# Rotary embedding in a decoder layer on one core: the two halves exchanged by a VectorE shuffle in place of a TensorE product, the cosine product on GpSimd

## What is computed

```python
def partial_rotary(x, pos):
    half = ROT_DIM // 2          # 8
    inv_freq = ROPE_THETA ** (-jnp.arange(half, dtype=jnp.float32) / half)
    ang = pos.astype(jnp.float32)[:, None] * inv_freq[None, :]
    cos, sin = jnp.cos(ang)[:, None, :], jnp.sin(ang)[:, None, :]
    xr = x[..., :ROT_DIM].astype(jnp.float32)
    x1, x2 = xr[..., :half], xr[..., half:]
    rot = jnp.concatenate([x1 * cos - x2 * sin, x2 * cos + x1 * sin], -1).astype(x.dtype)
    return jnp.concatenate([rot, x[..., ROT_DIM:]], -1)
```

## Time and profile before

| what | us |
|---|---|
| median of 3 runs | 1114.33 |
| lowest and highest | 1111.66, 1116.53 |
| profiled execution, its own time | 1120.03 |
| its span in the trace | 1118.0 |
| PE, DVE, ACT, POOL busy | 1066.5, 469.8, 225.4, 216.9 |
| rotation on DVE, first to last operation | 187.47 to 218.32 |

### The profile page before, as it was taken

How to read it: one execution, slowest core, us unless ns; L and a number is a source line. 1 busy time by engine, 2 the same in 40 slices (tenths; PEclk the granted TensorE clock), 3 DMA queues, 4 the chain that set the end, 5 groups by cost and what they waited for, 6 DMA issues and landing times. The chain is left out here.

```text
span 1118.0 us, 20957 instructions
## 1 busy us (share of the span) xinstructions
PE 1066.5 (95%) x8584; PEld 701.7 (63%) x8584; DVE 469.8 (42%) x939; ACT 225.4 (20%) x376; POOL 216.9 (19%) x193
## 2 busy tenths in 40 slices
PE   9999999999999899996999999999999999999980
PEld 8999998899997678874444444444444444444430
DVE  2799999800125728475232322121222212222215
ACT  3322221232225662011011010110101101101013
POOL 2354340232210014002111211211212112111010
PEclk9999999999898999996999999999999999999995
DMA  8377834146423521326999999999999999999614
GB/s 292 126 287 260 317 115 161 66 141 213 149 85 120 221 81 56 133 80 242 367 410 403 404 384 397 394 378 376 374 366 387 371 366 392 372 380 377 241 47 163
DMA packets 45681, 293.31 MB, mean 262 GB/s; under 512 B 11520, under 2 KB 15232, under 8 KB 26174
## 3 DMA queue, kind: packets, MB, share of 16 engines
q1 hardware_dynamic: 22285, 163.96, 38.0%
q10 hardware_dynamic: 12624, 102.63, 22.4%
q0 software_dynamic: 10720, 25.98, 7.8%
HBM read 286.83 MB, written 41.12 MB: 293 GB/s over the span
## 5 line engine op out<-in xcount | busy, mean ns | idle before, releaser
L1459 DVE SCALAR_TENSOR_TENSOR z_conv_gates<-scratch,column_vectors,z_conv_gates 128x512 f32<-128x512 f32 x240 | 138.6, 654 | 0.0
L998 PE MATMUL ps<-region_a,scratch 128*64 128x512 f32 x528 | 117.6, 594 | 0.0
L1038 PE MATMUL ps<-z_conv_gates,x_columns 128*64 128x512 f32 x512 | 116.9, 599 | 0.0
L587 PE MATMUL ps<-z_split,region_b_split 128*128 128x272 f32 x384 | 111.5, 290 | 2.0 <-ACT z_conv_gates L1119 2.0
L589 PE MATMUL ps<-z_split,region_b_split 128*128 128x272 f32 x384 | 111.8, 291 | 0.0
L588 PE MATMUL ps<-z_split,region_b_split 128*128 128x272 f32 x384 | 111.1, 289 | 0.0
L998 PE MATMUL ps<-region_b,scratch 128*64 128x512 f32 x496 | 111.1, 597 | 0.0
L1808 DVE SCALAR_TENSOR_TENSOR x_columns<-ps,column_vectors,x_columns 128x256 f32<-128x256 f32 x32 | 15.5, 484 | 198.5 <-ACT x_columns L1340 198.5
L998 PEld LDWEIGHTS ps<-region_a,scratch 128*64 128x64 f32 x528 | 36.9, 137 | 71.0 <-issue 71.0
L1913 POOL TENSOR_TENSOR region_b_split<-region_b,region_b_split 128x1024 fp32r<-128x1024 f32 x24 | 63.4, 2662 | 91.8 <-ACT region_b_split L1126 91.8
L1038 PEld LDWEIGHTS ps<-z_conv_gates,x_columns 128*64 128x64 f32 x512 | 33.9, 136 | 68.0 <-issue 68.0
(11 more groups left out here) (282 smaller groups left out, 1705.0 us busy)
## 6 DMA issues: line engine op xcount, KB each, us to landing
region_b<-in_gate_up_rows SPq DMA_DIRECT2D x21, 2048.0 KB, 29.6
region_a<-in_gate_up_rows ACTq DMA_DIRECT2D x21, 2048.0 KB, 29.8
z_conv_gates<-in_down_rows SPq DMA_DIRECT2D x32, 1024.0 KB, 12.6
z_conv_gates<-in_down_rows ACTq DMA_DIRECT2D x32, 1024.0 KB, 31.5
region_a<-in_gate_up_rows SPq DMA_DIRECT2D x12, 2048.0 KB, 29.1
region_b<-in_w_in_pairs SPq DMA_DIRECT2D x20, 1024.0 KB, 5.0
region_b<-in_gate_up_rows ACTq DMA_DIRECT2D x10, 2048.0 KB, 29.8
region_b<-in_cache_tiles POOLq DMA_DIRECT2D x16, 768.0 KB, 4.9
```

The costliest lines, as they stand in the source:

```text
L587: pe.matmul(out, w_hi[:, s, k, tile], x_hi[:, k, cols], start=k == 0, stop=False)
L998: last = pe.matmul(ps[half * BIG:(half + 1) * BIG, 2, :], ecols[s][:, 4 * c + k, 0:BIG], w[:, k, half, :], start=c + k == 0, stop=c + k == 4)
L1038: last = pe.matmul(ps[half * BIG:(half + 1) * BIG, 5, :], hcols_big[:, k % 2, k // 2, :], w[:, k, half * 512:(half + 1) * 512], start=k == ...
L1459: ve.scalar_tensor_tensor(dst, win(k), wdw_c[:, bass.ds(k * CT + c, 1)], dst, ALU.mult, ALU.add).then_inc(conv_step, 1)
```

## The change

The shuffle exchanges partitions p and p + 8 in the first 16 of each 32 partitions, from the q or k tile into `rtmp`. The sign moves into the table of sin, and the matrix `rot` goes. PE's step `rotate` is gone; its gate quarters stay in their places in the list. GpSimd has a new part in the step: the product with `cos`, in place, once the shuffle has read the tile (`rot_moved`). DVE adds for tile m - 1 behind the sin product of tile m; the shuffle of tile m waits for the add of tile m - 2, since `rtmp` has two places. PE's wait for the projection tiles and for the twelve adds goes to DVE: the first to the shuffle of tile 0, the second to the first copy of `values`. Line numbers of the changed kernel are some 2 to 13 lower ahead of L1480 and 7 lower in GpSimd's part before the new lines.

```diff
-            rot[h + j + half, h + j] = -1.0
-            rot[h + j, h + j + half] = 1.0
+            sin[h + j] = -sin[h + j]
...
-            def rotate(m):
+            def values_rows(m):
 
                 if m == 0:
 
                     pe.wait_ge(tile_free, 2 + 26)
-                if m >= 2:
-                    pe.wait_ge(rot_used, m - 1)
-                for half in range(2):
-                    last = pe.matmul(ps[:, 2 + 2 * (m % 2) + half, 0:HALF], rot, zqkv[:, m, half * HALF:(half + 1) * HALF],
-                                     start=True, stop=True)
-                last.then_inc(rot_ps, 1)
-
-            def values_rows(m):
-
-                if m == 0:
-                    pe.wait_ge(rotated, 12)
                 if m >= 3:
...
                 if m == 0:
                     ve.wait_ge(trig_loaded, 16)
-                ve.wait_ge(rot_ps, m + 1)
-                ve.tensor_tensor(v2(rtmp[:, m % 2, :]), ps[:, 2 + 2 * (m % 2):4 + 2 * (m % 2), 0:HALF], v2(sin), ALU.mult).then_inc(rot_used, 1)
-                link(ve.tensor_tensor(zqkv[:, m, :], zqkv[:, m, :], cos, ALU.mult))
-                ve.wait_ge(rot_used, m + 1)
-                ve.tensor_tensor(zqkv[:, m, :], zqkv[:, m, :], rtmp[:, m % 2, :], ALU.add).then_inc(rotated, 1)
+                    ve.wait_ge(tile_free, 2 + 26)
+                if m >= 2:
+                    ve.wait_ge(rotated, m - 1)
+                turned = rtmp[:, m % 2, :]
+                ve.stream_shuffle(out=turned, in_=zqkv[:, m, :], mask=[p + 8 if p < 8 else p - 8 if p < 16 else p for p in range(32)]).then_inc(rot_moved, 1)
+                ve.wait_ge(rot_moved, m + 1)
+                link(ve.tensor_tensor(turned, turned, sin, ALU.mult))
+                for n in ([m - 1] if m else []) + ([m] if m == 11 else []):
+                    ve.wait_ge(rot_cos, n + 1)
+                    ve.tensor_tensor(zqkv[:, n, :], zqkv[:, n, :], rtmp[:, n % 2, :], ALU.add).then_inc(rotated, 1)
 
             def value_rows(m):
                 if m == 0:
+                    ve.wait_ge(rotated, 12)
                     ve.wait_ge(gates_moved, 1)
...
+                if kind == "rotate":
+                    if i == 0:
+                        po.wait_ge(trig_loaded, 16)
+                    po.wait_ge(rot_moved, i + 1)
+                    po.tensor_tensor(zqkv[:, i, :], zqkv[:, i, :], cos, ALU.mult).then_inc(rot_cos, 1)
                 if kind == "rotate" and i == 11:
                     po.wait_ge(rotated, 12)
                     load_cache(3)
```

More of the change, by code:

```diff
@@ L73, in constants @@
     cos, sin = np.ones((P, N), np.float32), np.zeros((P, N), np.float32)
-    rot = np.zeros((P, P), np.float32)
     for h in range(0, P, HD):
@@ L100, in constants @@
         token[:, 0, i], token[:, 1, i] = 1 + i * P + p, i
-    return np.concatenate([cos, sin, eye, rot, before, rows, token.reshape(P, -1), pmask, smask], 1)
+    return np.concatenate([cos, sin, eye, before, rows, token.reshape(P, -1), pmask, smask], 1)
 C_COS, C_SIN = 0, N
 C_EYE = 2 * N
-C_ROWS = C_EYE + 3 * P
+C_ROWS = C_EYE + 2 * P
 NROWS = BLK + NBLK + NE + 2 * NTT
@@ L144, in build @@
         wa_t = sb("w_attn", 2048)
-        ci = sb("const_small", 3 * P + NROWS)
+        ci = sb("const_small", 2 * P + NROWS)
         colb = sb("column_vectors", 62 + TAPS * CT)
@@ L152, in build @@
         ps = ctx.enter_context(nc.psum_tensor("ps", [P, 8, 512], F32))
[L154 to L158, removed]
+        eye, before = ci[:, 0:P], ci[:, P:2 * P]
+        iota_r = ci[:, 2 * P:2 * P + BLK]
+        iota_b = ci[:, 2 * P + BLK:2 * P + BLK + NBLK]
+        iota_e = ci[:, 2 * P + BLK + NBLK:2 * P + BLK + NBLK + NE]
+        token = ci[:, 2 * P + BLK + NBLK + NE:].rearrange("p (k t) -> p k t", k=2)
         bdw_c, clg_c, clb_c, bco_c = (colb[:, i:i + 8] for i in (42, 46, 50, 54))
@@ L334, in build @@
         pads_set = sem("pads_set")
-        rot_ps, rot_used, rotated = sem("rot_ps"), sem("rot_used"), sem("rotated")
+        rot_moved, rot_cos, rotated = sem("rot_moved"), sem("rot_cos"), sem("rotated")
         state_sb = sem("state_sb")
@@ L841, in attend @@
                     turn(2 * p - 1)
-            work = dict(conv_rows=conv_rows, rotate=rotate, values=values_rows, sample_rows=sample_rows, keys=key_rows,
+            work = dict(conv_rows=conv_rows, values=values_rows, sample_rows=sample_rows, keys=key_rows,
                         cached_keys=cached_keys, new_keys=new_keys, conv_mean=conv_mean, conv_var=conv_var,
```

## The result

The changed kernel takes 1123.32 us (median of 4 runs, 1123.05 to 1125.35), the kernel before 1113.62 on the same occasion: a ratio of 1.0079, 95% interval 1.0063 to 1.0094. It is slower by 0.8%. Forecast were 1121.8 us and slower by 0.67%, with 0.73 on the side of slower; the range was 1117 to 1129.

What follows compares the result with a forecast made beforehand. TensorE was taken to bound the kernel: 18.4 us of new idle, less 10.2 saved and the earlier 0.2 wait, agreed within a microsecond with 7.5 us later; factor 1.0067 gave 1121.8 us, range 1117 to 1129.

Steps and rivals of the forecast that it cites:

- The turns of the two engines: Rotation: VectorE's two-SBUF-input operations and GpSimd's cos product do not overlap, so a step costs 3.30 us, before 2.6.
- rival 3: Rotation: GpSimd goes first each time, about 3.5 us a step, delay 10.5 us, 1124.8 us; chance 0.15.
- The shuffle: Rotation on VectorE: one pass over 544 columns, taken at 0.72 us; an estimate from the skill was 0.64.
- Rivals 2 and 4: Rotation's shuffle: dear at 1.44 us, over 1129 us, chance 0.08; or cheap at 0.44 us, 1119.3 us, chance 0.15.
- The length of the chain: Rotation on VectorE and GpSimd: runs from 187.5 to 228.8 us, its end 10.5 us later than before.
- Who waits: TensorE idles at gate tiles 4 and 5, values 3 and tile 6: 5.1, 8.2, 2.9 and 2.2 us.
- the two early waits: TensorE at gate tiles 4 and 5, for GpSimd's low halves behind cos products 4 and 8: 5.1 and 8.2 us.
- tile 6's low half: GpSimd's part of the gate weights, behind all 12 adds: ready at 232.1 us, making TensorE 7.5 us later.
- The sum: Whole kernel: TensorE 7.5 us later from tile 6 on, a factor of 1.0067, 1121.8 us.
- The clock: TensorE's granted clock likely falls after the new idle times; shows only if low behind 232 us, 3.4 us at most: 1125.
- Rival 1: Rotation: the engines overlap after all, a step 2.3 us, TensorE keeps 6.5 us, 1107.9 us; chance 0.12.

Runs made afterwards that it cites:

- the PSUM kernel: The changed kernel with the shuffle's result in PSUM, so sin product and add have one SBUF input each: 1110.42 us, ratio 0.9966 to the kernel before.
- The kernel with the early low halves: The changed kernel with GpSimd's low halves of gate tiles 4 and 5 moved ahead of cos products 2 and 4: 1123.83 us, ratio 1.009 to before.
- the later occasion: The changed kernel, unaltered, timed again on one chip with a kernel that adds unread TensorE products: 1126.79 us, ratio 1.0099 to the kernel before.
- the second trace: The kernel before, unaltered, run once more for another trace: 1114.10 us, ratio 1.0001 to before.

## Why the prediction held, and which terms were off

- *The turns of the two engines.* Right in mechanism and in size. A step was put at 3.30 us and is 3.35; cos products at about 1.9 and are 1.88; adds at about 1.9 and are 1.75, which the terms of the sum had said (1.33 + 0.58 - 0.13 - 0.04 = 1.74); the 1.9 was written down loosely. The sin product started first (0.04 against 0.09 us behind the shuffle), so rival 3 did not occur. The Trainium skill, page "SBUF — State Buffer", section "Who interferes with whom", states the rule that a VectorE instruction with two SBUF inputs and a GpSimd instruction that reads SBUF block each other, and one with at most one SBUF input does not contend. The trace agrees with the first half (1.88 us for 1.33), and the PSUM kernel with the second (1.34).
- *The shuffle.* Taken at 0.72 us, measured 0.76 from SBUF to SBUF (756 to 771 ns) and 0.72 into PSUM, with a further 14 ns ahead of each for its mask. The estimate of 0.64 us from the Trainium skill, page "VectorE: DVE Perf Modes", section "The perf-mode tier table", was 0.12 us low; the measurement decides. Rivals 2 and 4 fall with it.
- *The length of the chain.* 41.3 us forecast (187.5 to 228.8), 41.7 measured (186.1 to 227.8). Its start came 1.4 us and its end 1.0 us sooner than forecast.
- *Who waits.* TensorE waited four times as listed: 6.7, 6.4, 1.4 and 1.9 us, for 5.1, 8.2, 2.9 and 2.2. The sum stood on this: the two early waits don't matter, and tile 6's low half decides. The kernel with the early low halves confirms it.
- *The sum.* 7.5 us forecast; by the ratio it is 0.0079 x 1113.6 = 8.8 us, and by the 1.0099 of the later occasion 11.0 us, so the forecast was low both times. The term that was small is the distance from the chain's end before to its end after. I took its two ends from one trace: the chain of before ended at 218.32 there because TensorE ran 3.1 us late in that execution, and VectorE waited for its product of step 8 until 207.93, in the second trace until 204.80; VectorE's start was only 1.6 us late (187.47, and 185.89 in the second trace). In the changed kernel the chain is paced by VectorE's start. On the second trace the ends are 215.2 and 227.8, 12.6 us apart, not 10.5; less the 3.0 us that the low half had to spare, tile 6's quarter is 9.6 us later (221.5, now 231.1). With the clock that makes the 11.2 us at the cached keys. By the span's end it is 10.0 us; where the 1.2 us come back is not shown.
- *The clock.* It fell as said (0.59 from 200 to 205 us), and the price, "only if the level is still low behind 232 us, some 3.4 us at most", was 0 to 1.6 us.
- *Rival 1*, overlap and faster, was the behaviour of the PSUM kernel: 1110.42 where the rival had 1107.9. It needed VectorE operations with one SBUF input each, which the change did not give.

## What to carry to other kernels

Before an operation moves from VectorE to GpSimd, look at the inputs of what VectorE runs beside it: with two in SBUF the engines took turns here and the move only stretched both; with one of them in PSUM they overlapped. A product on the busiest engine may be what keeps a chain on the others hidden: when it goes, add up the chain to its end and find the last wait of the busiest engine that hangs on it. The largest wait need not be the one that costs: here the two early waits only took time from a later one. And take the distance between two engines' starts from more than one execution, since a late start of one of them moved the sum here by 2 us.

## What the runs showed of the hardware

- A shuffle of 128 x 544 f32 on VectorE takes 756 to 771 ns within SBUF and 723 to 729 ns into PSUM, and is recorded with a mask load of 14 ns ahead of it.
- With two SBUF inputs on VectorE, GpSimd's product of 1344 ns takes 1874 (median), and the waiting VectorE operation 1752 instead of 720; the turn goes to whoever starts first, here by 0.04 to 0.05 us, and passes 0.1 us ahead of the holder's recorded end.
- Such turns in twelve steps, the two low halves between them included, cost the chain 14.4 us (41.7 against 27.3), more than the 10.2 us of TensorE products that the change removed.
- The write does not matter: a sin product that reads PSUM and writes SBUF took 0.72 us beside GpSimd's product.
- The same kernel's two traces differ by 3.1 us at 166 us of the span: one has a wait of 2.0 us near 33 us and a stretch at 0.59 of the clock behind it, the other neither.
